# Pre-norm and transpose of the next layer moved into the output epilogue of the layer before

## The reference, cut to what matters

```python
def hybrid_layer(x, ...):
    h = rms_norm(x, pre_g)                 # x * rsqrt(mean(x^2)+eps) * pre_g
    z = h @ w_in                           # columns: q, k, v, g_a, p_in, g_b, s_u, s_v, g_c
    y_a = rms_norm(diff_attention(q, k, v, lam)) * (1 - lam_init)
    y_b = multi_scale_pool(p_in, ...)
    y_c = spatial_gating(s_u, s_v, ...)    # gelu(s_u) * (W_s layer_norm(gelu(s_v)) + b)
    branch = (each y * silu(its gate)) @ w_branch
    merged = sum(sigmoid(h @ w_merge + b_merge) * branch)
    out = merged @ w_out
    return x + rms_norm(out, post_g)       # becomes the x of the next layer
```

## Time and profile before

| | us |
|---|---|
| median of 3 runs | 1690.68 (1689.87 to 1691.19) |
| the profiled execution, its own time | 1689.05 |
| its span on core 0, first to last instruction | 1688.0 |
| the other cores of that execution | 1680.0 to 1687.9 |
| PE busy | 1480.2 (88%) |
| ACT busy | 762.9 (45%) |
| DVE busy | 743.5 (44%) |
| POOL busy | 340.5 (20%) |
| mean granted TensorE clock, core 0 | 0.958 of full |

### The profile page before, as it was taken

The page is one execution under the profiler, slowest core; times in us unless marked ns, Lnnn a source line. Parts: engine busy times, 40 slices in busy tenths (PEclk is TensorE's granted clock), DMA queues, the critical chain, the costliest instruction groups (busy, mean ns, idle before and its releaser), DMA issues.

```text
span 1688.0 us, 27635 instructions; the slowest of 8 cores (1680.0 to 1688.0 us)
## 1 busy us (share of the span) xinstructions
PE 1480.2 (88%) x8976; PEld 773.3 (46%) x9120; DVE 743.5 (44%) x1490; ACT 762.9 (45%) x1350; POOL 340.5 (20%) x297
## 2 busy tenths in 40 slices
PE   2898898879987999999828998988799989999997
PEld 1445566644433444444314465666444434444443
DVE  4424545457365223422444145554663652243224
ACT  5326676755453223322362266768454432233223
POOL 0000000004123333333300000000140333333343
PEclk9899999989998999999958999999899989999999
DMA  8311110100511434543230111101014114446442
GB/s 242 57 25 14 27 26 2 26 1 1 97 29 29 85 65 70 85 85 62 42 59 14 25 14 26 27 2 26 1 14 84 29 33 80 82 103 137 83 79 100
DMA packets 43355, 88.12 MB, mean 52 GB/s; under 512 B 2256, under 2 KB 33744, under 8 KB 39120
## 3 DMA queue, kind: packets, MB, share of 16 engines
q0 software_dynamic: 36592, 65.57, 23.7%
q1 hardware_dynamic: 6336, 20.12, 3.4%
q10 hardware_dynamic: 288, 0.66, 0.2%
HBM read 143.53 MB, written 8.39 MB: 90 GB/s over the span
## 4 chain that ended last, share of the span: by engine, by line
PE 76%; DVE 9%; issue 6%; ACT 3%; DMA 3%; POOL 2%; SPq 1%; DVEq 0%; ACTq 0%; POOLq 0%
PE PS L292 20%; PE PS L801 20%; PE PS L818 9%; PE PS L504 9%; PE PS L304 7%; PE PS L467 6%; PE PS L855 3%; POOL X L880 1%; DMA X<-x 1%; ACT JA L340 1%; PE PS L472 1%; PE PS L361 1%; DVE OT L874 1%; DVE VN L747 1%; DVE OUN L518 1%
## 5 line engine op out<-in xcount | busy, mean ns | idle before, releaser
L292 PE MATMUL PS<-HT,RING 128*128 128x512 bf16 x1718 | 396.1, 383 | 26.6 <-DVE QK L434 10.4
L491 ACT ACTIVATE PTB<-PS 128x512 bf16<-128x512 f32 x576 | 297.7, 573 | 127.5 <-PE PS L467 105.5
L801 PE MATMUL PS<-HT,RING 128*128 128x512 bf16 x1508 | 344.6, 383 | 6.6 <-DMA RING<-w_c 2.8
L805 ACT ACTIVATE GT<-PS,VPP 128x512 bf16<-128x512 f32 x192 | 131.5, 687 | 347.8 <-PE PS L801 347.7
L292 PEld LDWEIGHTS PS<-HT,RING 128*128 128x128 bf16 x1792 | 173.7, 99 | 224.1 <-issue 34.0
L504 PE MATMUL PS<-VA,PTB 128*128 128x130 bf16 x2176 | 220.9, 222 | 27.4 <-ACT PTB L491 10.4
L801 PEld LDWEIGHTS PS<-HT,RING 128*128 128x128 bf16 x1536 | 151.3, 99 | 189.6 <-issue 11.9
L467 PE MATMUL PS<-QK 128*128 128x256 bf16 (+1 forms) x1152 | 211.4, 270 | 0.0
L504 PEld LDWEIGHTS PS<-VA,PTB 128*128 128x128 bf16 x2176 | 146.1, 98 | 86.8 <-issue 56.7
L824 DVE TENSOR_TENSOR M<-PS,GT 128x512 f32<-128x512 f32 x64 | 44.3, 691 | 257.2 <-ACT GT L805 227.5
L830 POOL TENSOR_TENSOR M<-M 128x512 f32<-128x512 f32 x64 | 80.6, 1259 | 280.0 <-DVE M L827 262.9
(11 more groups left out here) (109 smaller groups left out, 1515.5 us busy)
## 6 DMA issues: line engine op xcount, KB each, us to landing
RING<-w_c POOLq DMA_DIRECT2D x32, 1152.0 KB, 9.4
RING<-w_in_p POOLq DMA_DIRECT2D x14, 1024.0 KB, 10.2
X<-x SPq DMA_DIRECT2D x16, 512.0 KB, 14.1
RING<-w_out_p POOLq DMA_DIRECT2D x8, 1024.0 KB, 8.7
y<-X SPq DMA_DIRECT2D x16, 512.0 KB, 2.7
RING<-w_in_p POOLq DMA_DIRECT2D x8, 512.0 KB, 5.4
GREP<-post_g_rep SPq DMA_DIRECT2D x2, 512.0 KB, 4.5
GREP<-pre_g_rep ACTq DMA_DIRECT2D x1, 512.0 KB, 7.0
```

The lines of the kernel that those rows point to most:

```text
L292: ins = pe.matmul(out=bank(b), lhsT=W[:, k, col0:col0 + 128], rhs=HTb(k, tb), start=(k == 0), stop=(k == 7))
L491: S.op("act", lambda: act.activation(out=PTB[:, pb_, :, c0:256], in_=Sb[:, :, c0:256], func=AF.Exp, scale=0.125), reads=[bankreg(sb)], wri ...
L801: ins = pe.matmul(out=bank(b), lhsT=W[:, (n * 8 + k) * 128:(n * 8 + k + 1) * 128], rhs=HTb(k, tb), start=(k == 0), stop=(k == 7))
L805: S.op("act", lambda n=n, b=b, gi=gi: act.activation(out=GT[:, gi, n, :], in_=bank(b), func=AF.Sigmoid, bias=pp(l, n * 8 + c)), reads=[ban ...
```

## The change

For layer 1 the stage A is no longer a stage of its own. A new function `fused_a_tile(t, ln)` computes square sum, root, reciprocal, scaling, transpose and the write to `HT` for one tile; it is called in the output projection of layer 0, for the tile before the one just emitted, and for the last tile of each half after the loop. In layer 1 only the 16 v tiles are left. The pre-norm gain is now applied at the write to `HT`, by DVE, from eight columns of `VPP`; so `GREP` holds the post-norm gain from the start of a layer. Layer 0 keeps its stage A, but in the new form: `a_tile` scales with one tensor operand, and the bank goes to `HT` by a DVE multiplication and not by an ACT copy. To make room, `RCNT` is loaded anew at the start of each B2 (by SP), `JC` becomes a view of `M0`, `TMPB` of B3 is replaced by four tiles of `GV`, and the lam products are written in place.

```diff
+    def fused_a_tile(t, ln):
+        S.op("act", lambda: act.activation(out=XSP[:], in_=X[:, t, :], func=AF.Square, accum_out=STA[:, t:t + 1]),
+             reads=[f"x{t}"], writes=["xsp", f"ssn{t}"])
+        S.op("act", lambda: act.activation(out=STA[:, 16 + t:17 + t], in_=STA[:, t:t + 1], func=AF.Sqrt,
+                                           scale=1.0 / D, bias=EPS), reads=[f"ssn{t}"], writes=[f"sqn{t}"])
+        S.op("dve", lambda: dve.reciprocal(out=STA[:, 32 + t:33 + t], in_=STA[:, 16 + t:17 + t]),
+             reads=[f"sqn{t}"], writes=[f"rstdn{t}"])
+        S.op("dve", lambda: dve.tensor_scalar(out=XSP[:], in0=X[:, t, :], scalar1=STA[:, 32 + t:33 + t], scalar2=None,
+                                              op0=ALU.mult), reads=[f"x{t}", f"rstdn{t}"], writes=["xsp"])
+        pb = rrA["b"] % 8
+        rrA["b"] += 3
+        PT_ = PS[:, pb, :].bitcast(BF16).rearrange("p (k n) -> p k n", k=8)
+        def tr():
+            for k in range(8):
+                ins = pe.transpose(out=PT_[:, k, :], in_=XSP[:, k * 128:(k + 1) * 128], identity=IDENT[:])
+            return ins
+        S.op("pe", tr, reads=["xsp", "ident"], writes=[bankreg(pb)])
+        S.op("dve", lambda: dve.tensor_tensor(out=HT[:, :, t * 128:(t + 1) * 128], in0=PT_, in1=pre_g_bc(ln),
+                                              op=ALU.mult), reads=[bankreg(pb), "vpp"], writes=[f"ht{t // 4}"])
...
-          S.dma("act" if l == 0 else "sp", "grep", GREP[:], pre_g_d[:, l, :], writes=["grep"])
+          S.dma("act" if l == 0 else "sp", "grep", GREP[:], post_g_d[:, l, :], writes=["grep"])
...
               def a_tile(t):
-                  S.op("dve", lambda: dve.scalar_tensor_tensor(
-                      out=XS[:, b, :], in0=X[:, t, :], scalar=ST2[:, 48 + t:49 + t], in1=GREP[:],
+                  S.op("dve", lambda: dve.tensor_scalar(
+                      out=XS[:, b, :], in0=X[:, t, :], scalar1=ST2[:, 48 + t:49 + t], scalar2=None,
...
-                  S.op("act", lambda: act.copy(out=HT[:, :, t * 128:(t + 1) * 128], in_=PT_),
+                  S.op("dve", lambda: dve.tensor_tensor(out=HT[:, :, t * 128:(t + 1) * 128], in0=PT_, in1=pre_g_bc(l),
+                                                        op=ALU.mult),
...
+              if l == 0:
...
+              else:
+                  for t in range(NT):
+                      v_tile(t)
...
-              S.dma("sp", "grep", GREP[:], post_g_d[:, l, :], writes=["grep"])
...
+                  S.dma("sp", "rcnt", RCNT[:], rcnt_d, writes=["rcnt"])      # start of B2, each layer
...
-                              tbf = rr["b"] % 2
-                              ... act.activation(out=TMPB[:, tbf, :], in_=bank(b), func=AF.Gelu) ...
+                              k = (tb * 4 + c) % 4
+                              ... act.activation(out=GV[:, k, :], in_=bank(b), func=AF.Gelu) ...
...
+                  JC = M0[:, 0, :].bitcast(BF16)[:, 0:512]                   # squares of L860 write region m0_0
...
                           if last:
                               S.dma("sp", "out", y_d[t * 128:(t + 1) * 128, :], X[:, t, :], reads=[f"x{t}"])
+                          elif tl >= 1:
+                              fused_a_tile(t - 1, l + 1)
+                      if not last:
+                          fused_a_tile(hf * 8 + 7, l + 1)
```

More of the change, by code:

```diff
@@ L19 @@
 SLOT = 4608
-NPP = 33
+NPP = 41
 class Region:
@@ L172, in build @@
     SW = nc.alloc_sbuf_tensor("SW", [128, 4, 128], BF16)
-    RCNT = nc.alloc_sbuf_tensor("RCNT", [128, 4, 16], F32)
     ST = nc.alloc_sbuf_tensor("ST", [128, 64], F32)
     ST2 = nc.alloc_sbuf_tensor("ST2", [128, 64], F32)
-    JL = nc.alloc_sbuf_tensor("JL", [128, 64], F32)
+    XSP = nc.alloc_sbuf_tensor("XSP", [128, D], BF16)
+    STA = nc.alloc_sbuf_tensor("STA", [128, 48], F32)
     MA = nc.alloc_sbuf_tensor("MA", [1, 128], BF16)
@@ L250, in pp, with pre_g_bc @@
         return VPP[:, l * NPP + j: l * NPP + j + 1]
+    def pre_g_bc(l):
+        return VPP[:, l * NPP + 33:l * NPP + 41].unsqueeze(2).to_broadcast([128, 8, 128])
+    rrA = {"b": 0}
+    def fused_a_tile(t, ln):
+        pe, act, dve = nc.tensor, nc.scalar, nc.vector
+        S.op("act", lambda: act.activation(out=XSP[:], in_=X[:, t, :], func=AF.Square, accum_out=STA[:, t:t + 1]),
[16 more added lines that the diff above has]
+                                              op=ALU.mult), reads=[bankreg(pb), "vpp"], writes=[f"ht{t // 4}"])
     open_stacks = []
@@ L372, in v_tile @@
                   proj_tm(Wv, wreg, t, 512, ev, banks=(2, 3, 4, 5))
[L373 to L386, removed]
+              if l == 0:
+                  a_stats(0)
+                  a_recip(0)
+                  for g in range(4):
+                      if g + 1 < 4:
+                          a_stats(g + 1)
+                      for t in range(4 * g, 4 * g + 4):
+                          a_tile(t)
+                      if g + 1 < 4:
+                          a_recip(g + 1)
+                      if g >= 1:
+                          for t in range(4 * g - 4, 4 * g):
+                              v_tile(t)
+                  for t in range(12, 16):
+                      v_tile(t)
+              else:
+                  for t in range(NT):
+                      v_tile(t)
               release_block()
               chk("A" + str(l), HT=HT[:])
-              S.dma("sp", "grep", GREP[:], post_g_d[:, l, :], writes=["grep"])
               open_stacks.pop().close()
@@ L591, in build @@
                       nc.sbuf_tensor(f"T16_{l}", [128, 16], F32) as T16, \
+                      nc.sbuf_tensor(f"RCNT_{l}", [128, 4, 16], F32) as RCNT, \
                       nc.sbuf_tensor(f"TMPB_{l}", [128, 2, 512], BF16) as TMPB:
                   ALLB = (0, 1, 2, 3, 4, 5, 6, 7)
+                  S.dma("sp", "rcnt", RCNT[:], rcnt_d, writes=["rcnt"])
                   W, wregp = next_block("PIN")
@@ L718, in ev @@
                           def ev(b):
[L719 to L721 removed]
+                              k = (tb * 4 + c) % 4
+                              S.op("act", lambda: act.activation(out=GV[:, k, :], in_=bank(b), func=AF.Gelu),
+                                   reads=[bankreg(b)], writes=[f"gv{k}"])
                               S.op("pool", lambda: pool.tensor_tensor(
                                   out=YC[:, c, tb * 512:(tb + 1) * 512], in0=YC[:, c, tb * 512:(tb + 1) * 512],
[L724 removed]
+                                  in1=GV[:, k, :], op=ALU.mult), reads=[f"gv{k}"], writes=[f"yc{c}_{tb}"])
                           proj_fm(Wsu, wregu, c * 128, tb, ev, banks=(4, 5, 6, 7))
```

23 lines of the change are left out of this document (10 added, 13 removed).

## The result

| | before | after |
|---|---|---|
| median of all runs, us | 1691.39 (10 runs) | 1803.04 (9 runs) |
| ratio, 95% interval | | 1.066 [1.065, 1.067] |
| profiled execution, us | 1689.05 | 1803.87 |
| its span, slowest core | 1688.0 (core 0) | 1802.7 (core 2) |
| its other cores | from 1680.0 | from 1791.4 |

The change costs 112 us; 1801 was forecast.

The account below looks back on a forecast made before the run. PE, busy 88% of the span, was taken as the bound. Terms 112.6 + 10.4 - 33.8 + 21.0 - 2 + 2 = +110.2 on 1689.05 gave 1799.3, as median 1801 us; range with rivals 1766 to 1838.

Parts of the forecast that it names:

- The wait of the transposes: Output projection of layer 0: PE idles from matmuls(t) until tile t's chain and t-1's scaling and transposes finish, 7.25 us.
- the other end, 1.28: Upper bound for the DVE scaling, taken at 0.70 us: 1.28 would add 0.58 on each of 32 scalings.
- The clock: Output projection of layer 0: each wait loses PE's full clock, +1.5 us a tile, ends 0 and +3.5.
- bank stall: Output projection of layer 0: tile 6 starts in bank 4, which the write to `HT` is still emptying, +1.5 us.
- First tile of a half: Output projection of layer 0: tile 0 delays tile 1 through the `M0` wait and the table load, +2.6 us.
- End of half 0: Layer 0: tile 7 runs in series before half 1's gates, which start at 11.15 us, +1.5 for clock; net +10.4.
- Between the layers: Last output matmul to last v matmul: ends at 56.2 us against 90.0, -33.8, with the `LAMV` chain now late.
- Stage A of layer 0: Scaling and `HT` write both on DVE, in series with transposes, 3.45 us a tile; stage ends at 108.6, +21.0.
- Small edits: `RCNT` hidden, `GV` -2 us over both layers, `M0` in layer 1 +2, lam in place 0: together 0.
- faster: Rival: PE does not wait in layer 0's output projection; decides at 2.4 us per wait; 1666 us, chance 3%.

Follow-up runs that it names:

- order experiment: Changed kernel with each tile's transposes emitted three output tiles later, with two buffers and PSUM banks 6 and 7 for them: 1718.28 us, ratio 1.017.
- useless products: Changed kernel with 22 unread matmuls on PE ahead of each tile's transposes, tiles 1 to 7 of each half of layer 0: 1779.60 us, ratio 1.059.
- `M0` alone: Kernel before with only `JC` made a view of `M0`: median 1696.47 us, ratio 1.0035.
- last run: Changed kernel with transposes three tiles later, old stage A in layer 0, lam chain behind the barrier, second X add on DVE: 1658.7 to 1659.3 us.
- two reordered kernels: Changed kernel, transposes three tiles later, old stage A in layer 0, lam chain moved: 1676.47 us with both X adds on POOL, 1658.7 to 1659.3 with one.

## Why the prediction was right, point by point

- *The wait of the transposes*, 7.25 us from the end of matmuls(t) to matmuls(t+1): 6.72 (695.52 to 702.24 in the kernel after). The order experiment shows its cause. The scaling was taken at 0.70 and took 0.753; the other end, 1.28, was wrong. The idle time ahead of the transposes is 5.91 for 6.10, and the next matmul starts 0.81 behind the first transpose and not 1.15.
- *The clock*, +1.5 a tile: 16 matmuls took 4.6 to 6.2 and not 3.46, +1.1 to +2.7, +1.9 on average. The two errors cancel, which is luck: a tile was to be 12.2 and was 12.1 on average without the bank stall (11.3 to 12.9). The useless products show the cause: they win 2.1 a tile where they keep the clock, 24 us in all.
- *First tile of a half* +2.6: 8.46 against 5.91. *Bank stall* +1.5: two of 1.5 (3.0 in all on L885). The halves: +56.4 for half 1, forecast 56.3.
- *End of half 0*: half 0 lost 66.7 (94.3 against 27.6) before half 1's gates and got 1.7 back in them; forecast 56.3 + 10.4 = 66.7, measured 64.9. (The terms of the 10.4 as written, 11.15 + 1.5 - 2.33, give 10.3.)
- *Between the layers* -33.8: 57.2 against 90.0, -32.8. The rule that what the removed stage had hidden comes out, held; `LAMV` took 9.84 and not 8.7.
- *Stage A of layer 0* +21.0: +18.0 (105.08 against 87.06). The tile is 3.22 and not 3.45. The old form gives the 18 back, in one execution.
- *Small edits* 0: this is the term that was mis-sized. `GV` gave nothing (forecast -2), and `M0` alone, on the kernel before, cost 6 and not 2: the forecast took +1 in each half of layer 1 and did not follow the delay to POOL's next weight load and to the clock behind it. Layer 1 behind its v stage is 7.8 us longer (768.7 on core 2 against 760.9), where the text said "as before" and +2. Of it 3.7 lie from the output projection of half 0 to that of half 1, where this edit acts, and 0.8 at the end. The rest, 2.3 in B1 and 1.0 in B2 and B3, is no larger than what the cores of one execution differ by, and is left open.
- Sum: 112.6 + 10.4 became 121.4; -33.8 became -32.8; +21.0 became +18.0; 0 became +7.8 and 0.3 in B1 to B3 of layer 0: 114.7, the difference of the two spans (1802.7 - 1688.0). The forecast had 110.2. The large terms were right in mechanism and within 3 us each; that the median is only 2 us off is luck too, since the misses (-1.6, +1.0, -3.0, +7.8) partly cancel and the two medians lie 3.2 us closer together than the two profiled executions.

Of the rivals, "faster" named the right place: with the wait at 0.6 us a tile, the fused kernel is faster than before. That takes another program order, and the last run changes stage A and the lam chain too, so the rival's threshold of 2.4 us a wait was not tested.

## What to carry to other kernels

When one engine hands work to another and waits for it, put that wait so much later in the program that the hand-over has had its time on every queue it passes: here one tile of delay was none, because the queues of DVE and ACT held tile t ahead of t-1, and three tiles of delay with two buffers won back 85 of 112 us. Where a stage is removed, ask what it hid. Where a scratch buffer is made a view of another to save room, follow the new wait to the next weight load and not only to the next reader. And count the clock: here each PE wait of 5.9 us cost another 2.1 us behind it.

## What the runs showed of the hardware

- A DVE scaling of 1024 float32 elements (one tensor operand) that begins beside a POOL addition of two float32 tensors is held, not slowed. It takes 0.753 us alone. In the two reordered kernels it took 0.77, 1.13 or 1.56 us, the longer the earlier it began beside the add, and on all cores, 224 times, it ended 0.55 us (0.548 to 0.554) behind the end of POOL's add. A rate that is only lower would not give one distance from that end.
- It works the other way too: POOL's second add, begun while the scaling was at work, took 1.53 us and not 1.27. And an addition of 128x1 on DVE took 1.22 us and not 0.15, ending within 0.02 us of that add.
- The Trainium skill ("SBUF — State Buffer", the shared port pair) has DVE and GpSimd take the same port by an exclusive lock for a whole instruction. The trace agrees on all three: each instruction that came second ran its course only behind the first.
- PE that multiplies for nothing through the wait keeps 2.4 GHz: the granted clock is 1.00 from 695 to 749 us in that run and 0.66 to 0.83 in the kernel after, the mean rose from 0.938 to 0.963, and the kernel was 24 us faster for it.
